# Attention stage: score products on two 64-row tiles, and the next head's sums of squares and roots moved to the end of a step

## The reference, cut to what matters

```python
q = _rmsnorm(aq.reshape(B, L, A_HEADS, 2, A_DH), qg)   # A_DH = 64, keys the same; then rotary on the latent tokens
s = jnp.einsum('bhcqd,bhckd->bhcqk', q, k) * (A_DH ** -0.5)     # c = 0, 1: the two halves of a head
p = jax.nn.softmax(s, axis=-1)
w = p[:, :, 0] - lam * p[:, :, 1]
o = jnp.einsum('bhqk,bhkd->bhqd', w, v)
y = _rmsnorm(o, sub_g) * (1.0 - lam_init)
```

## Time and profile before

| | before |
|---|---|
| median of 3 runs | 3147.98 us (3142.18 to 3152.9) |
| profiled execution | 3148.47 us |
| its span, first to last instruction | 3146.6 us |
| TensorE busy | 2731.3 us (87%) |
| VectorE busy | 1403.3 us (45%) |
| ScalarE busy | 930.7 us (30%) |
| mean granted TensorE clock | 0.963 of full |
| attention stage, layer 0, its eight steps | 381.6 to 642.2 us |
| attention stage, layer 1, its eight steps | 2052.6 to 2271.1 us |

### The profile page before, as it was taken

One profiled execution on the slowest core, in us unless ns is written; L12 is line 12 of the kernel. 1 busy time (PEld: TensorE's weight loads), 2 busy tenths in 40 slices (PEclk: granted clock), 3 DMA queues, 4 the chain that ended last, 5 costly groups with the idle time before them and its releaser, 6 DMA issues. The chain is left out here.

```text
span 3146.6 us, 40804 instructions
## 1 busy us (share of the span) xinstructions
PE 2731.3 (87%) x15578; PEld 1984.0 (63%) x15578; DVE 1403.3 (45%) x2560; ACT 930.7 (30%) x1615; POOL 0.2 (0%) x4
## 2 busy tenths in 40 slices
PE   5999999889998998987888878788789988987886
PEld 3887766567877766444444558766578886444444
DVE  5466655567454844111111566655474554111112
ACT  4223244433343332100000253344434443100001
POOL 0000000000000000000000000000000000000000
PEclk9999999999999998999999989999889998999999
DMA  6113411043111542999999322621062236999995
GB/s 230 73 67 122 162 41 40 27 167 121 67 67 41 205 164 103 428 429 398 416 428 429 119 87 87 237 81 53 26 245 92 81 134 248 428 429 428 428 429 217
DMA packets 59494, 635.11 MB, mean 202 GB/s; under 512 B 7854, under 2 KB 9840, under 8 KB 11376
## 3 DMA queue, kind: packets, MB, share of 16 engines
q1 hardware_dynamic: 59376, 633.55, 50.0%
HBM read 632.48 MB, written 1.05 MB: 201 GB/s over the span
## 5 line engine op out<-in xcount | busy, mean ns | idle before, releaser
L191 PE MATMUL ps<-rounded,rounded 128*128 128x256 f32 (+1 forms) x1856 | 640.8, 345 | 71.4 <-DVE rounded L182 36.8
L192 PE MATMUL ps<-rounded,rounded 128*128 128x256 f32 (+1 forms) x1856 | 629.8, 339 | 0.0
L193 PE MATMUL ps<-rounded,rounded 128*128 128x256 f32 (+1 forms) x1856 | 629.5, 339 | 0.0
L2219 PE MATMUL ps<-high_arena,low_arena 128*64 128x256 f32 x4288 | 497.9, 387 | 126.3 <-DMA high_arena<-in_e_w 97.9
L2219 PEld LDWEIGHTS ps<-high_arena,low_arena 128*64 128x64 f32 x4288 | 314.6, 139 | 331.3 <-DMA high_arena<-in_e_w 113.6
L182 DVE TENSOR_TENSOR rounded<-low_arena,rounded 128x1024 fp32r<-128x1024 f32 (+3 forms) x344 | 369.2, 1097 | 239.1 <-ACT rounded L178 234.8
L191 PEld LDWEIGHTS ps<-rounded,rounded 128*128 128x128 f32 x1856 | 361.7, 195 | 116.6 <-DVE rounded L182 35.6
L192 PEld LDWEIGHTS ps<-rounded,rounded 128*128 128x128 f32 x1856 | 362.0, 195 | 35.4 <-issue 0.5
L193 PEld LDWEIGHTS ps<-rounded,rounded 128*128 128x128 f32 x1856 | 361.2, 195 | 36.3
L178 ACT ACTIVATE rounded<-low_arena 128x1024 fp32r<-128x1024 f32 (+3 forms) x344 | 313.9, 950 | 195.5 <-PE ps L193 111.2
L167 PE MATMUL ps<-high_arena 128*128 128x256 f32 (+3 forms) x1072 | 264.3, 399 | 42.2 <-DVE high_arena L547 12.9
(11 more groups left out here) (383 smaller groups left out, 2743.9 us busy)
## 6 DMA issues: line engine op xcount, KB each, us to landing
high_arena<-in_e_w SPq DMA_DIRECT2D x201, 2048.0 KB, 25.4
low_arena<-in_d_wm SPq DMA_DIRECT2D x48, 1024.0 KB, 4.8
high_arena<-in_d_modlater SPq DMA_DIRECT2D x40, 1024.0 KB, 4.9
low_arena<-in_d_wml SPq DMA_DIRECT2D x32, 1024.0 KB, 4.9
low_arena<-in_d_wh SPq DMA_DIRECT2D x16, 1536.0 KB, 6.8
low_arena<-in_d_wa SPq DMA_DIRECT2D x16, 1536.0 KB, 6.6
low_arena<-in_d_wo SPq DMA_DIRECT2D x8, 1024.0 KB, 4.8
low_arena<-in_d_modfirst SPq DMA_DIRECT2D x3, 2048.0 KB, 29.6
```

Of the source, the lines that this page charges most:

```text
L191: pe.matmul(out, l_hi, r_hi, start=(k == 0), stop=False)
L192: pe.matmul(out, l_lo, r_hi, start=False, stop=False)
L193: last = pe.matmul(out, l_hi, r_lo, start=False, stop=(k == n - 1))
L2219: last = pe.matmul(K.ps[h * S:h * S + S, 4 * s + i, 0:HF], xg[s][:, k, :], w[:, k, h * HF:h * HF + HF], start=(k == 0), stop=(k == KC - 1))
```

## The change

- The score pair is computed from `qk[0]` and `qk[1]` directly, each half on its own 64 rows (rows 0 to 63, rows 64 to 127), without the zero-padded buffers. The four memsets, the two copies on ACT (layer 0) and one of two 64-row additions on DVE go with them; the remaining addition covers 128 rows.
- `sums(u + 1)` stands at the end of step u, between the last `turn` and `mix`, not at the start of step u + 1. The roots (`root(u + 1)`) on ACT follow the last copy of step u, and both squares stand ahead of that copy.
- PE's pieces are dealt out anew. Before `score(0)` of a step now stand eight value pieces and two query pieces. In layer 0 the four fillers behind `score(n)` are q 2 to 5; q 6, 7 and k 0, 1; k 2 to 5; k 6, 7. In layer 1 the two fillers are q 2 to 7 with k 0, 1; k 2 to 7.
- DVE splits the q weights of head u + 1 after `normed` of head u, and its k weights after the first query tile of head u. Before, both stood at the end of unit u - 1. In unit 0, and in the last unit, none is done there.

```diff
--- before.py
+++ after.py
@@ -1270,11 +1270,11 @@
     names = ("consts_in", "tile_in0", "tile_in1", "lam_step", "lam_sum", "q_projected", "k_projected", "v_projected",
              "squared", "v_copied", "summed", "rooted", "normed", "rotated", "roped", "scored", "maxed", "exped",
              "weighted", "turned", "copied", "mixed", "o_squared", "o_summed", "o_rooted", "unit_out", "chain", "acts",
-             "q_split", "zeroed", "root_logs", "o_logs", "w_rounded", "w_split", "vt_copied", "v_turned")
+             "root_logs", "o_logs", "w_rounded", "w_split", "vt_copied", "v_turned")
     with stage(nc, *names) as (consts_in, tile_in0, tile_in1, lam_step, lam_sum, q_projected, k_projected, v_projected,
                                squared, v_copied, summed, rooted, normed, rotated, roped, scored, maxed, exped,
                                weighted, turned, copied, mixed, o_squared, o_summed, o_rooted, unit_out, chain,
-                               acts, q_split, zeroed, root_logs, o_logs, w_rounded, w_split, vt_copied, v_turned), nc.Block() as block:
+                               acts, root_logs, o_logs, w_rounded, w_split, vt_copied, v_turned), nc.Block() as block:
         tile_in = [tile_in0, tile_in1]
         raw = [K.ring(s).rearrange("p (j k c) -> p j k c", j=3, k=KC) for s in range(2)]
 
@@ -1287,7 +1287,7 @@
         rs = [K.f(138, NTOK), K.f(140, NTOK)]
         qk = [[K.f(104 + 2 * s, NTOK) for s in range(2)], [K.f(108 + 2 * s, NTOK) for s in range(2)]]
 
-        qz = [[K.f(149 + 4 * s + 2 * c, NTOK) for c in range(2)] for s in range(2)]
+        head = [slice(c * A_DH, c * A_DH + A_DH) for c in range(2)]
         vt = [K.f(112 + 2 * s, NTOK).rearrange("p (t d) -> p t d", d=P) for s in range(2)]
         pr = [K.f(116 + 4 * s, 2 * NTOK).rearrange("p (c k) -> p c k", c=2) for s in range(2)]
         w = [K.f(124 + 2 * s, NTOK) for s in range(2)]
@@ -1369,11 +1369,10 @@
             def score(u, s, n):
                 q0, keys = qtiles[n]
                 if n == 0:
-                    pe.wait_ge(roped, u * 3 + 3)
-                    pe.wait_ge(q_split, u + 1)
+                    pe.wait_ge(roped, u * 2 + 2)
                 pe.wait_ge(exped, u * nq + n)
                 for c in range(2):
-                    last = pe.matmul(K.ps[:, 4 + c, 0:keys], qz[s][c][:, q0:q0 + P], qk[1][s][:, 0:keys],
+                    last = pe.matmul(K.ps[:, 4 + c, 0:keys], qk[0][s][head[c], q0:q0 + P], qk[1][s][head[c], 0:keys],
                                      start=True, stop=True)
                 last.then_inc(scored, 1)
 
@@ -1402,26 +1401,31 @@
                 v = (lambda *ks: project_v(u + 1, ks)) if more else (lambda *ks: None)
                 q, k = (lambda *ks: project(u + 1, 0, ks, q_projected), lambda *ks: project(u + 1, 1, ks, k_projected)) if more else (
                     lambda *ks: None, lambda *ks: None)
-                sums(u)
+                v(0, 1, 2, 3)
                 if not first:
                     o_sums(u - 1)
-                v(0, 1, 2, 3)
+                v(4, 5)
                 rotate(u, s)
-                v(4, 5, 6, 7)
+                v(6, 7)
+                q(0, 1)
                 score(u, s, 0)
-                pieces = [lambda: q(0, 1, 2, 3), lambda: q(4, 5, 6, 7), lambda: k(0, 1, 2, 3), lambda: k(4, 5, 6, 7)]
+
+                def fill(n):
+                    if nq == 4:
+                        (lambda: q(2, 3, 4, 5), lambda: (q(6, 7), k(0, 1)), lambda: k(2, 3, 4, 5), lambda: k(6, 7))[n]()
+                    else:
+                        (lambda: (q(2, 3, 4, 5, 6, 7), k(0, 1)), lambda: k(2, 3, 4, 5, 6, 7))[n]()
                 for n in range(nq):
-                    pieces[n]()
+                    fill(n)
                     if not more and n < 2:
                         gate_products(pe, K, l, 1, ahead, 0, range(4 * n, 4 * n + 4))
-                    if n == nq - 1:
-                        for piece in pieces[nq:]:
-                            piece()
-                    else:
+                    if n < nq - 1:
                         score(u, s, n + 1)
                     turn(u, n)
                     if n == 0 and more:
                         turn_v(u + 1)
+                if more:
+                    sums(u + 1)
                 mix(u, s)
 
             pe.wait_ge(lam_step, 2)
@@ -1432,6 +1436,7 @@
             project(0, 0, range(KC), q_projected, first_queries(K))
             project(0, 1, range(KC), k_projected)
             turn_v(0)
+            sums(0)
             step(0, 0, first=True)
             with pe.Fori(0, KC // 2 - 1) as i:
                 for s in range(1, 3):
@@ -1495,7 +1500,7 @@
                 act.wait_ge(o_logs, u + 1)
                 act.activation(ors[:, t0:], ors[:, t0:], ACT.Exp, scale=-0.5).then_inc(o_rooted, 1)
 
-            def step(u, s, first=False, more=True, then=True):
+            def root(u):
                 for j in range(2):
                     act.wait_ge(summed, u * 2 + j + 1)
                     t = slice(starts[j], NTOK)
@@ -1503,17 +1508,10 @@
                     act.activation(rs[j][:, t], K.ps[:, 4 + j, t], ACT.Ln, scale=1.0 / A_DH, bias=K.eps).then_inc(root_logs, 1)
                     act.wait_ge(root_logs, u * 2 + (j + 1))
                     act.activation(rs[j][:, t], rs[j][:, t], ACT.Exp, scale=-0.5).then_inc(rooted, 1)
+
+            def step(u, s, first=False, more=True, then=True):
                 if not first:
                     o_root(u - 1)
-                if ns == 2:
-
-                    act.wait_ge(normed, u * 2 + 1)
-                    if first:
-                        act.wait_ge(zeroed, 4)
-                    for c in range(2):
-                        part = slice(c * A_DH, c * A_DH + A_DH)
-                        last = act.activation(qz[s][c][part, 0:SEQ], qk[0][s][part, 0:SEQ], ACT.Copy)
-                    last.then_inc(q_split, 1)
                 if more:
                     copy_v(u + 1)
                 else:
@@ -1530,9 +1528,10 @@
                             weights(u + 2, s, 0, v_projected)
                 if more:
                     square(u + 1, 0)
+                    square(u + 1, 1)
                 copy(u, nq - 1)
                 if more:
-                    square(u + 1, 1)
+                    root(u + 1)
                 act.wait_ge(mixed, u + 1)
                 act.activation(osq[:, t0:], K.ps[:, 7, t0:], ACT.Square).then_inc(o_squared, 1)
                 if more and then:
@@ -1548,6 +1547,7 @@
             weights(1, 1, 1, q_projected)
             weights(1, 1, 2, k_projected)
             values(0, 0)
+            root(0)
             step(0, 0, first=True)
             with act.Fori(0, KC // 2 - 2) as i:
                 for s in range(1, 3):
@@ -1571,9 +1571,6 @@
             v.wait_ge(lam_step, 3)
             v.tensor_scalar(lam[:, 3:4], lam[:, 2:3], -lam_init, None, ALU.add).then_inc(lam_step, 1)
             v.wait_ge(lam_step, 4)
-            for s in range(2):
-                for c in range(2):
-                    v.memset(qz[s][c][A_DH - c * A_DH:P - c * A_DH, :], 0.0).then_inc(zeroed, 1)
             v.wait_ge(consts_in, 16)
             for j in range(3):
                 v.wait_ge(w_rounded, j + 4)
@@ -1595,20 +1592,16 @@
                     t = slice(starts[j], NTOK)
                     v.scalar_tensor_tensor(out=qk[j][s][:, t], in0=K.ps[:, j, t], scalar=K.cols[:, l, g:g + 1],
                                            in1=rs[j][:, t], op0=ALU.mult, op1=ALU.mult).then_inc(normed, 1)
+                rest = not first and not last
+                if rest:
+                    weights(u + 1, 1 - s, 1)
                 v.wait_ge(rotated, u + 1)
                 for j in range(2):
                     lat = qk[j][s][:, SEQ:]
                     ch.then(v.tensor_tensor(tmp[j], K.ps[:, 3, j * SEQ:j * SEQ + SEQ], rope[:, 1, :], ALU.mult))
                     ch.then(v.tensor_tensor(lat, lat, rope[:, 0, :], ALU.mult))
                     ch.wait()
-                    if j == 1:
-                        v.tensor_tensor(lat, lat, tmp[j], ALU.add).then_inc(roped, 1)
-                    else:
-                        for c in range(2):
-                            part = slice(c * A_DH, c * A_DH + A_DH)
-                            v.tensor_tensor(qz[s][c][part, SEQ:], lat[part, :], tmp[j][part, :], ALU.add).then_inc(roped, 1)
-                if ns == 1:
-                    v.sem_inc(q_split, 1)
+                    v.tensor_tensor(lat, lat, tmp[j], ALU.add).then_inc(roped, 1)
                 if not first:
                     output(u - 1)
                 if last:
@@ -1632,11 +1625,10 @@
                     ch.wait()
                     v.scalar_tensor_tensor(out=w[n % 2][:, 0:keys], in0=pr[n % 2][:, 1, 0:keys], scalar=st[:, n, 3, 1:2],
                                            in1=w[n % 2][:, 0:keys], op0=ALU.mult, op1=ALU.add).then_inc(weighted, 1)
+                    if n == 0 and rest:
```

(4 more changed lines are left out.)

## The result

The changed kernel takes 3128.67 us (median of five runs, 3127.17 to 3131.22) against 3147.98 us, a median of five runs too: a ratio of 0.994, 95% interval 0.9926 to 0.9955. It is faster by 19 us; the forecast was 3146, with a range from 3134 to 3160.

The account below looks back on a forecast made before the run. The order of waits, not any engine's load, was taken to bound the kernel. Layer 0 at -4.2 us and layer 1 at +2.5 gave -1.7 us against 3148.47, so 3146.8, stated as 3146 us; range 3134 to 3160.

Parts of the forecast that it names:

- C: Time of one score pair with 512 keys; taken as 1.29 us, between bounds of 1.72 and 0.86.
- the round trip: Score pair, maximum, exponentials, the same in both layers: 4.98 us before, forecast C + 3.26 = 4.55 us.
- rival C: All records of a score pair side by side, C = 0.86: total -13 us, 3135 us; chance 0.12.
- T: Moment the last product of `mix` has been issued; forecast T to T 33.33 us in layer 0, 28.5 in layer 1.
- S0: First score pair of a step; forecast 9.05 us after T in layer 0, 8.28 in layer 1.
- S1: Second score pair; forecast 4.55 us after S0 in layer 0, 8.75 in layer 1, there 10.05 before T.
- S2: Third score pair, layer 0; forecast 5.68 us after S1, with DVE's k split ahead of tile 1's maximum.
- S3: Fourth score pair, layer 0; forecast 5.05 us after S2, next T 9.0 us later with 1.4 us idle.
- rival B: Granted clock holds through layer 1's 3.6 us gap before the k products: 3137.5 us; chance 0.13.
- D: Low clock behind layer 1's gap lasts twice as long: another 1.4 us per step, 3155 us; chance 0.08.
- Rival A: The two halves of a score pair don't overlap, C = 1.72: total +10 us, 3158 us; chance 0.2.
- The drain: Tiling-mode changes at score pairs drain the array: two per pair, up to 0.3 us, sum up about 1 us.

Follow-up runs that it names:

- e3: Changed kernel with both products of a score pair on rows 0 to 63, the second half's scores replaced by the first's: 3168.61 us (one run).
- e5: Changed kernel with three idle 512-column products filling PE's gap in layer 1, between q piece 7 and k piece 0, steps 1 to 6: 3119.89 us, ratio 0.9907.
- e2: Changed kernel with the padded full-height score products of before, so the new order alone: 3167.1 us, ratio 1.006.
- e1: Kernel before with only the score products (on two 64-row halves), buffers and additions changed, order as before: 3121.78 us, ratio 0.9919.

## Why the prediction was wrong

**The step that failed is the price of the score pair.** I took C = 1.29 us, arguing that the two records of a product share their rows, so that only the middle two of four overlap. The pair showed the ends taken for a bound: 0.89 us by the round trip (4.15 less 3.26), 1.06 by PE's next start (554.57 to 555.63), which takes in the return to the full tile priced below. The halves run side by side from the start, in spite of the two records each; e3 shows that this, and not the 64 rows, is the cause. The argument had the records start in the order first half, first half, second half, second half; since two records on the same rows follow each other by 0.43 us or more in e3, the two that start 0.007 us apart must be of different halves. All side by side was rival C, given 0.12, and with it the sum would have been 3135. The rule that I set aside, of the Trainium skill (TensorE: Matmul & The Clock Gate, Packing small matmuls), puts a packed group at one matmul plus some 4 ns per tile. The trace agrees: the first records of the two halves start 0.007 us apart. The pair takes 1.13 us against 1.02 for two records in a row, but the 0.1 more is no price of the second half: four records of the padded pair take 1.98 us too, where four of L1360 take 1.88.

**Point by point, layer 0.** `rotate` 5.32 us after T (forecast 5.35), S0 9.12 after T (9.05). S0 to S1 4.15 (4.55, with C = 0.86 4.12). S1 to S2 5.53 (5.68): on DVE the split starts 0.08 us before the record ahead of it ends, and the maximum 0.08 before the split's end. S2 to S3 5.03 (5.05). S3 to T 8.8 (9.0). The idle time before the last `turn` was forecast as 1.4 and is 1.20. All but the pair held within 0.2 us.

**Layer 1.** S0 8.0 to 8.1 us after T (8.28). The gap before the k products, 3.4 us of the 3.6 forecast, released by L182. S0 to S1 8.7 to 9.7 and S1 to T 10.9 to 9.7, together 19.4 to 19.7 (forecast 8.75 and 10.05, with the clock's 1.5 20.3, and 19.4 with C = 0.86). The clock fell in each of six steps and cost 1.5 us (forecast 1.4 to 1.5), as e5 shows; rival B, that it holds, falls, and so does D, since the step would have been another 1.4 longer. The steady step came to 27.65, 0.35 more than before, where rival C's sum has 0.4.

**What was left over.** With C = 0.86 the stages were to give 13 us; they gave 16.3. Steps 1 to 6 of layer 0 gave 1.0 each instead of 0.7, and the last step of layer 1 gave 5.5 us (27.3 to 21.8) instead of some 4, as the clock did not fall in it before S0. The other 4.8 us of the spans lie outside the stages and can't be told from the scatter there. The range was too narrow: it ended 1 us beyond rival C's own sum and left nothing for this scatter.

**Rival A** (no overlap, 3158) is what e2 and e3 build: 3167 and 3169. Its mechanism was priced 9 us too low: in e2 a pair behind the gap, at the lower clock, takes 3.2 us, not 1.98, which the sum didn't have and which makes 7 of the 9 over six steps.

**The drain.** TensorEngine Tiling (Array Packing) of the Trainium skill, Key Properties, says that a change of mode drains the array. The trace agrees in so far as PE loses 0.16 us per pair on the way back to the full tile (e3 against e2). That is what the prediction took for one change; it named two per pair, and left both out of the sum. In e3 the 0.16 us are gone again at S3; whether they cost anything elsewhere in the changed kernel, no run here shows.

## What to carry to other kernels

A price between two far bounds, multiplied by every step, decides a forecast; where no row shows it, the range must reach past the sums of both ends by the scatter of the rest of the program (here 12 us over eight kernels). When a step of preparation is moved on one engine, look for the first instruction that needs it on each other engine and for what is queued behind that: here one split of 1.22 us, put a few lines lower, held up the next score pair, let the clock fall in layer 1, and took two thirds of what the change could give (3091 us against 3129). Two moves that are timed together should be timed apart, as a good one can hide a bad one; and their prices need not add, as e1 and e2 show.

## What the runs showed of the hardware

Two float32 products of 64 rows each, on rows 0 to 63 and 64 to 127 and into different PSUM banks, take 1.13 us together with 512 columns; one after the other on the same rows 1.98. With the pair on 64 rows the next work on the full tile starts 0.16 us later than behind a pair on the full tile (e3 against e2).

Idle time of 3.4 to 3.6 us on PE was followed by a mean granted clock of 0.50 to 0.67 over the next 3.5 us, in all six steady steps of the changed kernel and in three steps each of e2 and e3; 0.8 us in the same place (e5) was not. Idle time of 2.4 us ahead of S0 in the last steps of the changed kernel had the clock low for the pair in layer 0, and in layer 1 only behind it. Shorter idle time is no safe side: with 1.4 us ahead of S1 the clock fell in three of six steady steps of e1, with 1.6 us in none of the six of the kernel before. What tells these cases apart is open.
